# A two-layer hybrid mixer on one core: low parts, output weights and one Fourier wait in another order

## The reference

```
h = rmsnorm(x) * (1 + scale) + shift
q, k, v, z (branch A), u, z (branch B), q, k, v, z (branch C), g = split(h @ w_in)
o_na = neighbourhood_attention(...)                  # branch A
o_f  = real(fft2(u over positions, channels)) @ fnet_w   # branch B, 4 channel groups of 128
o_d  = differential_attention(...)                   # branch C
y = sum over b of sigmoid(g_b) * ((o_b * silu(z_b)) @ w_branch[b])
x = x + gate * (y @ w_out)
```

## Time and profile before

| | before |
|---|---|
| median of 3 runs | 2963.04 us (2957.88 to 2968.26) |
| the profiled execution, as timed | 2963.45 us |
| its span in the profile | 2961.4 us |
| busy: PE | 2885.4 us (97%) |
| busy: DVE | 1334.4 us (45%) |
| busy: ACT | 1076.3 us (36%) |
| busy: POOL | 615.0 us (21%) |
| share of the chain that ended last: PE | 90% |

### The profile page before, as it was taken

The page is one execution under the profiler, slowest core; times in us unless marked ns, Lnnn a source line. Parts: engine busy times, 40 slices in busy tenths (PEclk is TensorE's granted clock), DMA queues, the critical chain, the costliest instruction groups (busy, mean ns, idle before and its releaser), DMA issues.

```text
span 2961.4 us, 44076 instructions
## 1 busy us (share of the span) xinstructions
PE 2885.4 (97%) x18396; PEld 2764.1 (93%) x18396; DVE 1334.4 (45%) x2291; ACT 1076.3 (36%) x1947; POOL 615.0 (21%) x312
## 2 busy tenths in 40 slices
PE   6999999999999999999999999999999999999998
PEld 4999999999999989999999999999999989999987
DVE  4343443123557575446344344421156567554543
ACT  4333333221444444412343343323134444433122
POOL 0221221122211211112331221212221221211132
PEclk9999999999999999999999999999999999999999
DMA  5332223102111102253421121220211111215522
GB/s 212 112 109 82 102 90 136 66 15 78 48 41 46 48 32 97 97 197 124 137 77 62 66 82 39 93 82 22 77 33 47 48 41 46 86 54 180 173 90 94
DMA packets 84277, 248.55 MB, mean 84 GB/s; under 512 B 9200, under 2 KB 30192, under 8 KB 83056
## 3 DMA queue, kind: packets, MB, share of 16 engines
q1 hardware_dynamic: 84080, 245.74, 24.2%
HBM read 191.71 MB, written 54.00 MB: 83 GB/s over the span
## 4 chain that ended last, share of the span: by engine, by line
PE 90%; DVE 5%; ACT 2%; DMA 1%; issue 1%; SPq 0%; POOL 0%; DVEq 0%; POOLq 0%; ACTq 0%
PE ps L728 44%; PE ps L711 18%; PE ps L821 6%; PE ps L767 6%; PE ps L898 3%; PE ps L1040 3%; PE ps L1031 2%; PE ps L956 2%; PE ps L886 2%; PE ps L938 1%; DVE e L1838 1%; DVE stat L1821 1%; ACT e L1434 1%; DMA wmod<-w_mod 1%; DVE aTl L1845 1%
## 5 line engine op out<-in xcount | busy, mean ns | idle before, releaser
L728 PE MATMUL ps<-hhi,whi 128*128 128x384 f32 x2640 | 916.4, 347 | 5.7 <-DVE obuf L1853 3.3
L728 PE MATMUL ps<-hhi,wlo 128*128 128x384 f32 x2640 | 886.2, 336 | 0.0
L728 PE MATMUL ps<-hlo,whi 128*128 128x384 f32 x2640 | 884.1, 335 | 0.0
L1956 POOL TENSOR_TENSOR wlo<-wraw,whi 128x1024 fp32r<-128x1024 f32 (+1 forms) x188 | 416.9, 2218 | 2068.4 <-ACT whi L1126 2068.4
L728 PEld LDWEIGHTS ps<-hhi,whi 128*128 128x128 f32 x2640 | 500.0, 189 | 24.1 <-issue 7.3
L728 PEld LDWEIGHTS ps<-hlo,whi 128*128 128x128 f32 x2640 | 497.0, 188 | 0.9
L728 PEld LDWEIGHTS ps<-hhi,wlo 128*128 128x128 f32 x2640 | 496.0, 188 | 0.0
L1126 ACT ACTIVATE whi<-wraw 128x1024 fp32r<-128x1024 f32 (+1 forms) x188 | 174.5, 928 | 230.8 <-PE ps L711 212.7
L1443 ACT ACTIVATE aTh<-ps 128x512 fp32r<-128x512 f32 (+1 forms) x200 | 96.5, 483 | 278.6 <-PE ps L1031 278.6
L1690 DVE TENSOR_TENSOR ptl<-ps,pth 128x512 fp32r<-128x512 f32 (+1 forms) x144 | 82.1, 612 | 246.8 <-ACT pth L1300 246.6
L1821 DVE TENSOR_REDUCE stat<-ps 128x1 f32<-128x1152 f32 x144 | 176.6, 1231 | 16.9 <-PE ps L767 16.1
(11 more groups left out here) (199 smaller groups left out, 4857.6 us busy)
## 6 DMA issues: line engine op xcount, KB each, us to landing
wraw<-w_in SPq DMA_DIRECT2D x128, 512.0 KB, 4.2
gates_dram<-gst SPq DMA_DIRECT2D x48, 576.0 KB, 3.1
gth<-gates_dram SPq DMA_DIRECT2D x48, 576.0 KB, 4.8
mraw<-w_mod SPq DMA_DIRECT2D x32, 512.0 KB, 3.7
wraw<-w_branch SPq DMA_DIRECT2D x48, 256.0 KB, 2.7
bias<-rpb SPq DMA_DIRECT2D x8, 1280.0 KB, 6.3
outs_dram<-obuf SPq DMA_DIRECT2D x16, 576.0 KB, 4.2
oraw<-outs_dram SPq DMA_DIRECT2D x16, 576.0 KB, 3.7
```

Source lines behind the costliest of these rows:

```text
L728: x = mm(ps[:, bank, 0:CH], a[:, s % 2, k, :], b[:, k, n * CH:(n + 1) * CH], start=(k == 0 and a is whi and b is hhi), stop=(k == KT - 1 a ...
L1956: g_.tensor_tensor(lo[:, 0:kt, :], wraw[:, n % 2, 0:kt, :], hi[:, 0:kt, :].bitcast(F32), ALU.subtract).then_inc(S.w_lo, 1)
```

## The change

There are three edits, each in both layers.

The first is in the Fourier stage. The waits for the tables and for the evacuation of `u` g go from ahead of the job into `pair(g, 0)`, and those ahead of `z` 0 and `z` 1 go away.

The second is in the branch and output projections. DVE does `y_low` of row m - 1 at the head of step m of the last branch, ahead of the evacuation of row m, so that only row 7 is left after the loop. PE takes units 0 and 1 of the output up to row 6, and then row 7 of both.

The third is in SP's list. At the first unit the weights up to that of unit 4 are issued ahead of residual 4; at unit m of chunk 0, the weights of units up to m + 5 are issued behind residual m + 4, in place of those up to m + 2 ahead of it. Chunks beyond unit 7 are the first ones of the next layer.

```diff
                 for i in range(NC * KT):
                     n, m = divmod(i, KT)
-                    if n == 0:
-                        weights_to(CHUNK["o", l, "", m] + 3)
+                    if i == 0:
+                        weights_to(CHUNK["o", l, "", 0] + 5)
                     if i + 4 < NC * KT:
                         old_load(i + 4)
+                    if n == 0:
+                        weights_to(CHUNK["o", l, "", min(m + 3, KT - 1)] + 3)
...
                 def pair(g, j):
 
                     n = l * HEADS + g
+                    if j == 0:
+                        pe.wait_ge(S.tab_load, 96 * (l + 1))
+                        pe.wait_ge(*evacuated("u", l, "fn", g))
                     if j < 2 and g:
...
-                pe.wait_ge(S.tab_load, 96 * (l + 1))
-                pe.wait_ge(*evacuated("u", l, "fn", 0))
                 job(("u", l, "fn", 1), hhi, hlo, None, over_channels(0))
                 job(("u", l, "fn", 2), hhi, hlo)
                 pe.wait_ge(*evacuated("u", l, "fn", 1))
...
-                pe.wait_ge(*evacuated("u", l, "fn", 2))
                 job(("z", l, "fn", 0), hhi, hlo, None, over_channels(2))
                 pe.wait_ge(S.q_done, 2 * (l * HEADS + 2))
                 over_tokens(2)
-                pe.wait_ge(*evacuated("u", l, "fn", 3))
                 job(("z", l, "fn", 1), hhi, hlo, None, over_channels(3))
...
                 for m in range(2):
-                    out_unit(l, 0, m, 0, 6)
+                    out_unit(l, 0, m, 0, KT - 1)
                 for m in range(2):
-                    out_unit(l, 0, m, 6, KT)
+                    out_unit(l, 0, m, KT - 1, KT)
...
                     n = l * 3 * KT + i
+                    if i > 2 * KT:
+                        y_low(m - 1)
                     dve.wait_ge(g_load[n % 3], 16 * (n // 3 + 1))
                     dve.wait_ge(S.w_used, SPLIT_NO["b", l, "", i] + 1)
...
-                    if i >= 2 * KT + 2:
-                        y_low(i - 2 * KT - 2)
-                y_low(KT - 2)
                 y_low(KT - 1)
```

## The result

The changed kernel took 2940.5 us, the median of 3 runs (2938.72 to 2941.24), against 2963.04: a ratio of 0.9928 [0.9915, 0.9941]. The intervals of all ratios here are some 0.26% wide, mostly because the runs of the kernel before spread over ten us.

A forecast was written before the change was run, and what follows sets the result against it. The prediction took TensorE (PE), busy nearly the whole span, as the bound. Gains of 1.3 + 3.0 + 7.3 + 9.8 = 21.4 us off the profiled 2963.45 gave 2942 us, range 2935 to 2953.

The forecast's parts named there:

- Fourier wait: First Fourier stage, job `u` 1: moving the wait gains 1.3 us in layer 0 and 3.0 in layer 1.
- The rival that the whole stall moves: Fourier stage: the whole stall moves into pair(0,0) or pair(0,2), 4.3 us missing, 2946 us; chance 0.05.
- the 4.3: Both layers' Fourier stage: the gains of 1.3 and 3.0 us, missing if the whole stall only moves.
- Low parts: End of last branch pass: low parts ahead of next evacuation, row 7 alone left; PE waits 0.3 us for it.
- The order on the port: Rival, DVE and POOL at row 6: POOL's split goes first, costing 2.9 us a layer, 2948 us; chance 0.04.
- the end of the range that held it like the add: Last evacuation beside POOL's split: 1.5 us a layer if held like the add; 0 was taken.
- Unit 2 starts at 1405.7, after a new wait of 1.2 us: Output of layer 0: unit 2 waits for POOL's weight split, in place of starting at about 1408.4.
- Output weights: Output projection: weights issued ahead of residual chunks, no wait at unit 3; output gains 7.3 us in layer 0, 9.8 in layer 1.
- the rival of slow transfers: Output weights land in 5.8 us instead of 3.65, costing 1.8 us a layer, 2946 us; chance 0.07.
- the slower rival: SP's queue: residual chunks go out too late, each late unit paying some 3 us, about 2968 us; chance 0.03.
- The slow stretch at unit 3: Output, both layers: matmuls running slow around unit 3 before the change give 1.45 us a layer back.
- Half clock after the short waits: Rival: each of PE's four short stops brings a slow stretch of 2.65 us, up to 10.6, 2953 us; chance 0.11.

The follow-up runs named there:

- the run with the weights first: Changed kernel with the weights of `u` 2 issued ahead of SP's wait for the evacuation of `u` 0 and two rope tables: 2938.8 us.
- The undoing: Changed kernel with the Fourier waits put back ahead of the job: 2946.02 us; the same kernel in a later set: 2942.41 and 2942.78 us.
- the last two kernels: Changed kernel with Fourier waits put back, 2942.41 and 2942.78 us; changed kernel with scale factors later and weights of `u` 2 first, 2936.79 us.

## Why the prediction was right, by its steps

**Fourier wait: right in both layers.** The forecast did not credit the whole stall, because the fold on DVE hangs on a transfer that the change leaves where it is. ACT's and DVE's timelines after:

```profile
548.66 1.06 ACT L1127 ACTIVATE whi<-wraw 128x1024 fp32r<-128x1024 f32 x1 [6.33 <-DMA wraw<-w_in]
```

```profile
550.36 0.41 DVE L1741 TENSOR_TENSOR xdif<-xcs,ps 128x256 f32<-128x256 f32 x1
```

From the landing to the end of the fold it is 550.77 - 548.66 = 2.11, the distance of the earlier trace rows, and PE starts 0.06 later. Waits of 1.11 and 1.09 against 1.1 and 1.0. The rival that the whole stall moves is out (4.1 gained), and the run with the weights first shows where the rest was. In the 3.0 of layer 1 there is luck all the same: 1.5 of it is the slow stretch behind the stall (26.21 before, 24.68 in layer 0), which the forecast took over from one profile as if it always came. The undoing shows it in both layers of one execution and in neither of another, so the 4.3 could as well have been 2.9 or 5.8.

**Low parts: right, with two small misses.** Row 7 was to make PE wait 0.3; no wait is recorded, and the gap in front of 1400.31 is about 0.04 more than the step of 0.17. PE came there 0.2 later than forecast because it stood that long, until 1396.50, ahead of unit 1, whose weights POOL had split only at 1396.44. The order on the port did not turn round: the low part of row 6 began 1.49 ahead of POOL's split (1392.56 and 1394.05), with a forecast margin of 1.47. The evacuation beside POOL's split cost nothing, so the end of the range that held it like the add is out, and the last add took 2.38, held to the end of POOL's split as forecast. All 32 of the kernel (ns) after, against the earlier trace rows:

```profile
L1911 DVE SCALAR_TENSOR_TENSOR gth<-gth,ps x32: 1346/1354/1355, 1298.6 to 2820.1; 128x1152 f32<-128x1152 f32 x32
```

The miss: **"Unit 2 starts at 1405.7, after a new wait of 1.2 us"**. Counted from the output's start that is 9.97 us. It came 10.62 after it in layer 0 and 9.89 in layer 1. I followed POOL alone and left out that the scale factors stand between the last low part and the evacuations: 0.65 more in layer 0. The Trainium skill, "SBUF — State Buffer", section "Who interferes with whom", has the rule that the first of the two to issue holds the port for its whole instruction. The trace agrees for an instruction of 0.16 us as for the adds: two of them took 2.42. The forecast weighed that rule for the adds and not for these.

**Output weights: right.** The weights of unit 3 go out at 1396.47, 3.8 after the output's start; the wait ahead of unit 3 is gone, and no unit behind it waits. The transfers take what they took alone, so the rival of slow transfers is out; issues in 1395 to 1412 us after, KB each and median us to landing:

```profile
wraw<-w_out SPq DMA_DIRECT2D x4, 512.0 KB, 3.6
xold<-x_in SPq DMA_DIRECT2D x3, 192.0 KB, 3.8
```

The landing of 5.8 in that rival was not even what its rule gives: 3.65 for 512 KB and two chunks of 192 KB at the same rate are 6.4. The residual chunks went out behind the weights, and no evacuation waited for one, which rules out the slower rival.

**The slow stretch at unit 3 was taken too small.** It was 1.45 a layer. In the chain that ended last, PE's piece from unit 3 of layer 1 has 135 matmuls in 25.65 us before, and the piece from unit 2 has 159 in 28.22 after:

```profile
2854.57 25.65 PE ps L821 x135
```

```profile
2828.86 28.22 PE ps L823 x159
```

At 28.22 / 159 = 0.1775 each the 135 would take 23.96, so the slow stretch cost 1.69. With the start of unit 3 in layer 1 at 2828.86 + 24 x 0.1775 = 2833.12, 14.15 after the output's start instead of 22.65, that is 8.5 + 1.7 = 10.2, the measured 10.22 (forecast 8.4 + 1.45). In layer 0 the 135 matmuls took 25.76 before, 1.8 more. Unit 3 starts there at about 1407.6, 14.9 after the output's start instead of 20.10: 5.2, and with 1.8 that is the 7.01. Two errors of opposite sign, 0.6 for the scale factors and 0.3 for the clock, make 7.01 of 7.3; that it came so near is luck in part.

**Half clock after the short waits: out.** No matmul behind the four waits of 0.9 to 1.6 runs slow, in any of the three profiles of the changed kernel, and the stretches are at 1.00. Against that, stops of 2.31 and 3.54 us did bring 1.2 GHz in runs that undid a part; the one of 3.37 without SP's part did not, nor the one of 3.53 for the low part of row 5 in layer 0 of the kernel before. Where it came, undoing a part costs more than its idle time.

**Not in the forecast:** what differs from run to run without any edit, the 2.60 ahead of job `u` 0 and the -0.80 between the Fourier stage and the output of layer 0. The wait for split weights at the first branch job holds 0.34 of the -0.80 (0.40 before, 0.74 after). Of the 22.5 between the medians the forecast explains 21.3 in the profiles; the rest is not assigned.

## What to carry to other kernels

When a wait on a busy engine is moved, find what ends second there and follow it back to an event that the change does not move: here a weight transfer, and it took half of the stall. Where two engines block each other, list everything that stands in the program between the last instruction of one job and the first that matters of the next, the tiny ones too: 0.23 us of scale factors became 2.4. Compare the kernels piece by piece at the same instructions, since the start of the program alone moves by up to 4 us from profile to profile. And when a slow stretch of the clock behind a stall goes into a sum, give it a range: it need not come in the next execution.

## What the hardware showed unexpectedly

A DVE instruction of 8 elements a partition was held for a whole POOL split (2345 ns instead of 160), while an evacuation with one operand in PSUM ran beside such a split in 1.35 us, as without it (the split took its usual 2.39). A waiting DVE add went ahead of POOL's next split although POOL had that one ready (3.51 instead of 2.39). And the clock after equal stops of 2.31 us of one kernel was 1.2 GHz in one execution and 2.4 in another. The changed kernel does the same at the start of layer 1, where no edit is: PE's timelines of its first profile and of that beside the last two kernels have a stop of 2.44 there, and the stretch from it to job `u` 0 took 428.99 in the one and 427.45 in the other. That a stop of one length goes either way was seen; why was not found.

```profile
1526.03 0.65 PE L730 MATMUL ps<-hhi,whi 128*128 128x384 f32 x1 [2.44 <-POOL wlo L1956]
```

```profile
1525.70 0.44 PE L730 MATMUL ps<-hhi,whi 128*128 128x384 f32 x1 [2.44 <-POOL wlo L1956]
```
